# Experts' third token round: two experts of each four, over 64 tokens, on all four column strips

## What is computed

```python
logits = jnp.einsum('btd,de->bte', h, P['moe_router'][i])
probs = jax.nn.softmax(logits, axis=-1)
top_p, top_i = lax.top_k(probs, TOP_K)                      # TOP_K = 2
top_p = top_p / jnp.sum(top_p, axis=-1, keepdims=True)
gate = jnp.sum(jax.nn.one_hot(top_i, N_EXPERTS) * top_p[..., None], axis=-2)
hg = jnp.einsum('btd,edf->btef', h, P['moe_w_gate'][i])     # 8 x 1024 x 1792
hu = jnp.einsum('btd,edf->btef', h, P['moe_w_up'][i])       # 8 x 1024 x 1792
a = jax.nn.silu(hg) * hu * gate[..., None]
return jnp.einsum('btef,efd->btd', a, P['moe_w_down'][i])   # 8 x 1792 x 1024
```

## Time and profile before

| | |
|---|---|
| median of 3 runs | 1883.8 us (1882.7 to 1884.61) |
| profiled execution: its time, its span | 1880.36 us, 1878.4 us |
| TensorE busy | 1821.2 us, 97% of the span |
| VectorE, ScalarE, GpSimd busy | 34%, 19%, 8% |
| TensorE's granted clock, mean | 0.99 of full speed |
| DMA moved | 563.94 MB, 300 GB/s over the span |
| gather(0) to scatter(1) on TensorE | 1355.3 to 1870.6 us |

### The profile page before, as it was taken

How to read it: one execution, slowest core, us unless ns; L and a number is a source line. 1 busy time by engine, 2 the same in 40 slices (tenths; PEclk the granted TensorE clock), 3 DMA queues, 4 the chain that set the end, 5 groups by cost and what they waited for, 6 DMA issues and landing times.

```text
span 1878.4 us, 30169 instructions
## 1 busy us (share of the span) xinstructions
PE 1821.2 (97%) x12741; PEld 1295.9 (69%) x12741; DVE 644.2 (34%) x1394; ACT 366.0 (19%) x754; POOL 154.2 (8%) x259
## 2 busy tenths in 40 slices
PE   8999999999999999999999989999799999999998
PEld 5889888786688999888888878777433343433434
DVE  3444441527337665353544233452400000000000
ACT  2141333332000000015124332310110000100001
POOL 3000000404100110000000020320000000000000
PEclk9999999999999999999999999999799999999999
DMA  9933599989999998897349998997649999599992
GB/s 273 284 116 112 198 312 330 356 316 382 374 347 386 347 325 284 306 377 255 120 150 313 312 362 297 354 384 276 240 156 370 362 391 403 200 360 385 374 408 110
DMA packets 263162, 563.94 MB, mean 300 GB/s; under 512 B 11965, under 2 KB 160673, under 8 KB 262752
## 3 DMA queue, kind: packets, MB, share of 16 engines
q1 hardware_dynamic: 243696, 500.14, 74.1%
q0 software_dynamic: 18544, 58.58, 9.1%
q10 hardware_dynamic: 784, 3.25, 0.5%
HBM read 547.74 MB, written 196.63 MB: 396 GB/s over the span
## 4 chain that ended last, share of the span: by engine, by line
PE 93%; DMA 3%; DVE 2%; issue 1%; ACT 1%; POOL 0%; ACTq 0%; DVEq 0%; POOLq 0%
PE PS L902 33%; PE PS L1538 16%; PE PS L1564 8%; PE PS L1334 7%; PE PS L1310 4%; PE PS L1342 4%; PE PS L822 3%; PE PS L946 3%; PE PS L1324 2%; PE PS L1500 2%; PE PS L939 2%; PE PS L1586 1%; PE PS L1246 1%; PE PS L1220 1%; PE PS L837 1%
## 5 line engine op out<-in xcount | busy, mean ns | idle before, releaser
L902 PE MATMUL PS<-h,ring 128*128 128x264 f32 x2816 | 654.2, 389 | 0.0
L902 PEld LDWEIGHTS PS<-h,ring 128*128 128x128 f32 x2816 | 527.8, 191 | 106.8 <-issue 21.5
L1703 ACT COPY z<-PS 128x264 f32<-128x264 f32 (+3 forms) x307 | 130.6, 444 | 854.2 <-PE PS L902 527.8
L1538 PE MATMUL PS<-ring,z 128*32 128x512 f32 (+1 forms) x1440 | 212.2, 527 | 1.2 <-ACT z L1703 1.2
L1538 PE MATMUL PS<-arena,z 128*32 128x512 f32 (+1 forms) x1056 | 190.1, 535 | 0.0
L1538 PEld LDWEIGHTS PS<-ring,z 128*32 128x32 f32 x1440 | 68.5, 111 | 126.9 <-issue 111.4
L1564 PE MATMUL PS<-arena,z 128*32 128x512 f32 x432 | 104.0, 592 | 0.0
L1538 PEld LDWEIGHTS PS<-arena,z 128*32 128x32 f32 x1056 | 55.0, 110 | 53.5 <-issue 53.4
L1310 PE MATMUL PS<-z,ring 128*128 128x264 f32 x384 | 87.3, 388 | 0.0
L1538 PE MATMUL PS<-z 128*32 128x512 f32 x576 | 84.7, 593 | 0.0
L1564 PE MATMUL PS<-ring,z 128*32 128x512 f32 x480 | 83.5, 592 | 0.0
(11 more groups left out here) (357 smaller groups left out, 2192.4 us busy)
## 6 DMA issues: line engine op xcount, KB each, us to landing
out_win_s<-in_cache_win_kv SPq DMA_DIRECT2D x128, 1023.5 KB, 12.0
ring<-in_w_in SPq DMA_DIRECT2D x88, 1024.0 KB, 7.5
out_win_s<-in_cache_win_kv SPq DMA_DIRECT2D x32, 1022.0 KB, 12.4
ring<-in_moe_w_gate SPq DMA_DIRECT2D x28, 1024.0 KB, 9.6
arena<-in_moe_w_up SPq DMA_DIRECT2D x22, 1024.0 KB, 11.6
ring<-in_moe_w_up SPq DMA_DIRECT2D x22, 1024.0 KB, 8.8
ring<-in_moe_w_down SPq DMA_DIRECT2D x20, 1024.0 KB, 11.1
arena<-in_moe_w_down SPq DMA_DIRECT2D x18, 1024.0 KB, 10.4
```

The source lines that it names most:

```text
L902: last = mm(bank(l, "p", j)[:, 0:T], w[:, k, P * (j % 2):P * (j % 2) + P], h[:, k, :], start=(k == 0), stop=(k == KT - 1))
L1538: last = mm(m_bank("c", "gu", g, b, w, r)[BLK * j:BLK * j + BLK, 0:n], hs[:, k, P * r + BLK * j:P * r + BLK * j + BLK], v3(slot_ap(set_slo ...
L1703: return nc.scalar.copy(out, in_)
```

## The change

The first two rounds stay as they are (FULL = 64 tokens of each expert). The third serves only PAIR = 2 experts of the four, those with more than 64 tokens. Each of them gets two strips, one for the left and one for the right half of the weight columns, so that a third-round matmul has 256 columns (128 in the block of 256) in place of 512. In the down part its two output halves lie on two strips, in one PSUM bank (five `dn` banks in place of six). A group has SLOTS = 320 slots in place of 384.

Which two experts these are is known only at run time. VectorE reads their numbers into registers (`which`) and copies their part of each set, in two pieces of 1024 columns for each of the two, from the set's place to two fixed tiles `over[0]` and `over[1]` (`bring`); TensorE reads them there (`over_piece`). The semaphores `over_in` and `over_used` pass the tiles to and fro, one piece at a time. So that a register can address the chunk, the four chunks of a set now lie next to each other: ring and arena are one tile `mem`, and the third set place is in the tail of `z` (`set_slots`). The third round's turn-overs are two in place of four, ScalarE copies them in one or two parts (`turned`), and two ST tiles more are turned back, eight in all. In `route` VectorE also finds which experts are over 64 and whether more than two of a four are (then `crowded` is set too); `find_slots` and `weigh_slots` build G and `gw` with wide instructions.

Not shown below: new places of some tiles in memory, one semaphore in place of two for `relb_in` and for `r_gate`, the list of PSUM banks, and the order of ScalarE's `slots_back`.

```diff
+FULL = (ROUNDS - 1) * BLK
+PAIR = 2
+SLOTS = QUAD * FULL + PAIR * BLK
...
+        def unended(n):
+
+            ended = [t for t in range(SET_EG) if GU_SETS[t][2] != 0] + [SETS - 1]
+            return n - sum(1 for g in range(2) for t in ended if 2 * (SETS * g + t) + 1 < n)
...
+        ztail = z.rearrange("p a b -> p (a b)")[:, Z_N * T - QUAD * CW:Z_N * T]
...
+        def set_slots(t):
+
+            if t % 3 < 2:
+                return v3(mem[:, QUAD * (t % 3) * CW:QUAD * (t % 3 + 1) * CW], QUAD)
+            return v3(ztail, QUAD)
...
+        over = [small[:, 0:D], cm.take(D)]
...
-                            last = mm(m_bank("c", "gh", g, d + w)[:, 0:QUAD * CAP], htok[i][0:nt, P * (d + w):P * (d + w) + P],
-                                      G[0:nt, i, g].rearrange("p r j s -> p (r j s)"), start=(i == 0), stop=(i == 2))
+                            last = mm(m_bank("c", "gh", g, d + w)[:, 0:SLOTS], htok[i][0:nt, P * (d + w):P * (d + w) + P],
+                                      G[0:nt, i, g, :], start=(i == 0), stop=(i == 2))
...
-                for i in range(BLOCKS[b][1] // P):
+                for i in range(BLOCKS[b][1] // P // (1 if u % ROUNDS < 2 else PAIR)):
...
+            def over_piece(g, t, p, out, tokens, ks, kt):
+
+                n = 2 * (SETS * g + t) + p
+                pe.wait_ge(over_in, n + 1)
+                wide = out.shape[1]
+                for k in ks:
+                    for s_ in range(QUAD):
+                        a_, half = s_ // 2, s_ % 2
+                        last = mm(out[BLK * s_:BLK * s_ + BLK, :], tokens[:, k, QUAD * FULL + BLK * a_:QUAD * FULL + BLK * a_ + BLK],
+                                  v3(over[a_], len(ks))[:, k - ks[0], wide * half:wide * half + wide],
+                                  start=(k == 0), stop=(k == kt - 1))
+                        if k == ks[-1] and s_ == QUAD - 2 and t >= SET_EG and p == 1 and t < SETS - 1:
+                            last.then_inc(sets_used, 1)
+                return last
 
             def hidden_chosen(g):
...
-                    for r in range(ROUNDS):
+                    for r in range(2):
...
-                        if part == 0:
-                            continue
-                        last.then_inc(m_done("c", "gu", g, b, w, r), 1)
-                        if w and b + r:
-                            turn_hidden(g, ROUNDS * b + r - 1)
-                    if g == 0 and 2 <= t < 8:
+                        if part != 0:
+                            last.then_inc(m_done("c", "gu", g, b, w, r), 1)
+                            if w and b + r:
+                                turn_hidden(g, ROUNDS * b + r - 1)
+                        if not part and r == 0:
+                            m_open(pe, "c", "gu", g, b, w, 2)
+                        half = ks[r * len(ks) // 2:(r + 1) * len(ks) // 2]
+                        last = over_piece(g, t, r, m_bank("c", "gu", g, b, w, 2)[:, 0:n // 2], hs, half, KT)
+                        if part != 0 and r == 1:
+                            last.then_inc(m_done("c", "gu", g, b, w, 2), 1)
+                        else:
+                            last.then_inc(over_used, 1)
+                    if w and part != 0:
+                        turn_hidden(g, ROUNDS * b + 1)
+                    if g == 0 and 2 <= t < 10:
...
-                        for n in range(2 * ROUNDS):
+                        for n in range(4):
...
-                    if q < SET_ED - 1:
-                        last.then_inc(sets_used, 1)
+                        if k == 0:
+                            m_open(pe, "c", "dn", g, 4)
+                        last = over_piece(g, SET_EG + q, w, m_bank("c", "dn", g, 4), fc, range(k, k + 1), FE // P)
...
-                    for r in range(ROUNDS):
-                        last = mm(m_bank("c", "fd", g, d)[:, 0:T], ys[:, r, P * d:P * d + P], ST[:, ROUNDS * g + r, :],
-                                  start=(r == 0), stop=(r == ROUNDS - 1))
+                    out = m_bank("c", "fd", g, d)[:, 0:T]
+                    for r in range(2):
+                        mm(out, ys[:, r, P * d:P * d + P], ST[:, QUAD * g + r, :], start=(r == 0), stop=False)
+                    last = mm(out, ys_over[:, P * (d % 4):P * (d % 4) + P], ST[:, QUAD * g + 2 + d // 4, :],
+                              start=False, stop=True)
                     last.then_inc(m_done("c", "fd", g, d), 1)
...
+                if r == 2:
+                    n = n // P // PAIR
+                    for i in range(n):
+                        last = copy(fc[:, c0 // P + i:c0 // P + i + n + 1:n, QUAD * FULL:SLOTS].rearrange("p f (a s) -> p a f s", a=PAIR),
+                                    m_bank("c", "tf", g, u)[:, P * i:P * i + P].rearrange("p (a f s) -> p a f s", a=PAIR, f=2))
+                    last.then_inc(m_read("c", "tf", g, u), 1)
+                    return
...
+                counts = bank(1, "rc", 0)[:, 0:NE]
+                ts(rover, counts, float(FULL) + 0.5, None, ALU.is_gt)
+                link(nc.vector.tensor_reduce(rmost[:, 0:1], counts, AX.X, MAX))
+                dve.drain().then_inc(free(1, "rc", 0), 1)
+                ts(rmost[:, 1:2], rmost[:, 0:1], float(CAP) + 0.5, None, ALU.is_gt)
+                for g in range(2):
+                    last = nc.vector.tensor_tensor_scan(rorder[:, QUAD * g:QUAD * g + QUAD], ones[:, 0:QUAD],
+                                                        rover[:, QUAD * g:QUAD * g + QUAD], 0.0, MUL, ADD)
+                link(last)
+                link(nc.vector.tensor_reduce(rmost[:, 2:3], rorder, AX.X, MAX))
+                link(stt(rmost[:, 0:1], rmost[:, 2:3], float(PAIR) + 0.5, rmost[:, 1:2], ALU.is_gt, ADD))
+                ts(crowded[0:1, 0:1], rmost[0:1, 0:1], 0.5, None, ALU.is_gt).then_inc(r_flag, 1)
+                for a_ in range(PAIR):
+                    last = stt(rsel[:, a_].rearrange("p g j -> p (g j)"), rorder, float(a_ + 1), rover, ALU.is_equal, MUL)
...
+            def find_slots(g):
+
+                for r in range(2):
+                    tt(G[:, :, g, P * r:P * r + P].rearrange("p i (j s) -> p i j s", j=QUAD),
+                       ranks(1 + BLK * r).to_broadcast([P, 3, QUAD, BLK]),
+                       bc(rpos[:, :, QUAD * g:QUAD * g + QUAD], 3, [P, 3, QUAD, BLK]), ALU.is_equal)
+                over_rows(g, rpos)
+                tt(third(G[:, :, g, 2 * P:SLOTS]), ranks(1 + FULL).to_broadcast([P, 3, PAIR, BLK]),
+                   bc(rab, 3, [P, 3, PAIR, BLK]), ALU.is_equal)
+                dve.drain().then_inc(r_slots, 1)
+
+            def weigh_slots(g):
...
+            def weigh_slots(g):
+
+                link(nc.vector.memset(gw[:, :, g, 2 * P:4 * P], 0.0))
+                over_rows(g, rg)
+                for r in range(2):
+                    tt(gw[:, :, g, P * r:P * r + P].rearrange("p i (j s) -> p i j s", j=QUAD),
+                       G[:, :, g, P * r:P * r + P].rearrange("p i (j s) -> p i j s", j=QUAD),
+                       bc(rg[:, :, QUAD * g:QUAD * g + QUAD], 3, [P, 3, QUAD, BLK]), MUL)
+                for half in range(2):
+                    at = 2 * P + P * half
+                    tt(gw[:, :, g, at:at + P].rearrange("p i (a f s) -> p i a f s", a=PAIR, f=2)[:, :, :, half, :],
+                       third(G[:, :, g, 2 * P:SLOTS]), bc(rab, 3, [P, 3, PAIR, BLK]), MUL)
+                dve.drain().then_inc(r_back, 1)
 
...
+                which = [[dve.value_load(crowded[0:1, 1 + 2 * a_ + g:2 + 2 * a_ + g], min_val=0, max_val=QUAD - 1)
+                          for a_ in range(PAIR)] for g in range(2)]
+
+                def bring(g, t, p):
+
+                    n = 2 * (SETS * g + t) + p
+                    if p == 0:
+                        for j in range(QUAD):
+                            s_ = set_slot(t, j)
+                            dve.wait_ge(landed[s_], 16 * (loads[s_] + (SETS * g + t) // 3 + 1))
+                    before = n - 1
+                    if before >= 0:
+                        g_, t_, p_ = before // (2 * SETS), before // 2 % SETS, before % 2
+                        if p_ and t_ == SETS - 1:
+                            m_wait_full(dve, "c", "dn", g_, 4)
+                        elif p_ and t_ < SET_EG and GU_SETS[t_][2] != 0:
+                            m_wait_full(dve, "c", "gu", g_, *GU_SETS[t_][0:2], 2)
+                        else:
+                            dve.wait_ge(over_used, unended(n))
+                    for a_ in range(PAIR):
+                        last = cp(over[a_], set_slots(t)[:, bass.DynSlice(which[g][a_], 1), D * p:D * p + D].rearrange(
+                            "p a b -> p (a b)"))
+                    last.then_inc(over_in, 1)
+
+                def gate_up(g, u):
+
...
+                    w = BLOCKS[b][1] // (1 if r < 2 else PAIR)
...
+                bring(0, 0, 0)
                 for g in range(2):
-                    for u in range(ROUNDS * len(BLOCKS)):
```

(42 more changed lines are left out.)

105 lines of the change are left out of this document (60 added, 45 removed).

## The result

The changed kernel takes 1848.76 us in the median of four runs (1848.23 to 1849.26). The kernel before, run beside it on the same chip, takes 1883.25 us, and the ratio is 0.9827, with a 95% interval of 0.9815 to 0.9839. The profiled execution took 1848.23 us around a span of 1846.1 us. The forecast was 1855 us with 1847 to 1868 as its range, by transfers that become the limit.

The account below looks back on a forecast made before the run. TensorE was taken to set the pace, with DMA transfers within half a microsecond a set. Savings of 9.8 + 14.2 + 6.2 - 1.7 = 28.5 us gave 1851.9, plus 3.4 for the median 1855 us, range 1847 to 1868.

Parts of the forecast that it names:

- What bounds the kernel: Expert part: TensorE sets the pace, but transfers have no room either; the two limits stand within half a microsecond a set.
- The transfers' chain: Hidden and down parts: group time built from first issue, transfers and last set; saves 14.2 us in group 0, 9.8 in group 1.
- TensorE's 73 us: All 42 sets: the gain at 1.74 us a set were TensorE alone the limit; with gathers 1804 us, a rival given 2%.
- The lighter set: Each weight set: half-width third-round matmuls cut TensorE's time by 1.74 us to 8.72 us.
- Gather: Both gathers: 320 columns in place of 384, at 290 ns an instruction, save 6.2 us (5.6 to 6.6).
- VectorE: Four new copies per set: a pair fits under TensorE's main round of 3.49 us, so they cost 0.
- the upper row: VectorE's copies: upper bound of 1.15 us a copy, read from a TENSOR_TENSOR operation at 1.08 ns an element.
- the lower row: VectorE's copies: lower bound of some 0.8 us a copy, read from a TENSOR_SCALAR of 128x528 taking 436 ns.
- C: TensorE in the sets: half clock does not end; 1910 us at 12.2 us a set; 4%, 6% more for a part.
- D: Staging tiles: a copy pair over 4.5 us stalls TensorE; gain gone at 4.9, 1929 us at sets of 12.7; 4%.
- The clock: TensorE after waits in each set: half clock shows only in a group's last set, 1.7 us; half of two, +1.7 us.
- The signs named ahead: Profile after: DMA waits of 1 to 2.5 us in most sets, about 25 a group; DMA idle between groups about 12.

Follow-up runs that it names:

- e1: Changed kernel with only the first half of each expert weight chunk transferred, all computation kept: 1798.57 us, ratio 0.9581.
- e2: Kernel before the change with only the first half of each expert weight chunk transferred: 1877.57 us, ratio 0.9985.
- e5: Changed kernel with each pair of VectorE copies made three times in a row: 1859.91 us, ratio 0.9894.
- e3: Changed kernel without VectorE's copies, TensorE reading the two experts' chunks in place at addresses written into the program: 1847.25 us, ratio 0.9822.
- e6: Changed kernel with each pair of VectorE copies made four times in a row: 1975.32 us, ratio 1.0521.
- e11: The changed kernel itself, measured again for comparison on one chip: 1846.87 us, ratio 0.9825.
- e7: Changed kernel with the scatter of group 0 spread, one tile behind each of sets 1 to 8 of group 1: 1837.01 us, ratio 0.9778.
- e10: The same kernel as e7, measured again beside the changed kernel on the same chip: 1839.12 us, ratio 0.9782.
- e8: Changed kernel with each gather cut in two, half before the group's first set and half behind it: 1844.12 us, ratio 0.9803.
- e9: Changed kernel with both the spread scatter of group 0 and the two gathers cut in two: 1839.60 us, ratio 0.9791.
- e4: Changed kernel without VectorE's copies and with only half of each expert weight chunk transferred: 1799.75 us, ratio 0.957.

## Why the prediction was right, point by point

*What bounds the kernel.* Shown: by e1 against e2 the change is worth 79 us without the transfers' limit and 35 with it, and while a group loads the DMA share stays at 1.04.

*The transfers' chain.* Forecast for group 1: 9.6 + 1.6 + 194.7 + 8.9 = 214.8 us. Measured: the first issue at 1622.68, which is 9.6 after 1613.08; bytes from 1624.3, 1.6 later; 192.9; then 9.03, in sum 213.15. Group 0 has 11.3 + 1.6 + 193.1 + 9.0 = 215.0 where 216.5 was forecast. What was off is the rate, above all that of the gate and up sets, 392 in place of 384 GB/s, and that is 3.1 us in both groups together. Why it rose is open. It is not that TensorE now waits: e5, where a set takes 10.5 us and TensorE waits for no DMA, has 391. Nor is it the copies, since e3 has 393 without them. The chunks also lie at new places in memory, and that was not tried alone. That the sum came out of the DMA's own chain, and not out of TensorE's 73 us, made the forecast.

*The lighter set.* 8.72 us was forecast, 8.58 measured. In the 256-column block the pieces of 128 columns cost less again (32 in 1.01 us), which I had left open; as said, nothing hangs on it.

*Gather.* 290 ns an instruction were read off the line between 264 and 384 columns; 14.48/48 = 302 ns were measured in gather(1), above the proportional 296 too. Gather(0) saved 1.9 us, as it again ran at half clock at first. Both gave 4.4 of the 6.2 us, below the 5.6 to 6.6 of the forecast.

*VectorE.* Cost zero, as forecast. I took the upper row, 1.15 us; a copy is 0.69, below even the 0.8 of the lower row. The Trainium skill says that an operation with one source in SBUF uses both read ports and goes twice as fast even in fp32, which one with two tensors can't ("VectorE: DVE Perf Modes", Mode 2×_2P); the trace agrees in kind, with 0.67 ns an element here against 1.08 in the earlier trace rows, 1.6 times as fast and not twice. The page would have named the lower row as the near one. It decides nothing at one pair, but by the upper row the three pairs of e5 would have taken 6.9 us, more than the 5.3 of e6's four.

*The prices of C and D.* They are some 25 us too low. By their figures, 1910 for sets of 12.2 us and 1929 for 12.7, both take 1855 us for a set of 10.9 and add from there. But the kernel before has sets of 10.84 us on average (455.3/42), so at 10.9 only the gathers' gain is left. Summed as for e5, sets of 12.7 give 42 x 12.7 = 533 us, 78 more than 455.3, less 6.2 for the gathers: 1956. D would have begun to lose near 11.0 us a set, a pair of 4.6 us and not 4.9, and part of the gain goes well before, as e5 shows at 4.0. The forecast doesn't use these prices, and it stands.

*The clock.* +1.7 us was forecast, none came. Windows of the kernel after, behind three of the waits for DMAs and, in the last row, at the begin of hidden(0), behind 1.2 us for ScalarE:

```profile
1670.00:1673.00 3.00, 3.00 (x19) 0.90 (x15) 0.61 (x2) 0.00 (x0) 0.00 (x0) 0.51 1.05 385
1735.00:1738.00 3.00, 2.49 (x24) 1.35 (x28) 1.63 (x3) 0.00 (x0) 0.00 (x0) 0.50 1.09 346
1496.00:1499.00 3.00, 2.62 (x28) 1.44 (x32) 1.62 (x3) 0.00 (x0) 0.00 (x0) 0.50 1.10 348
1372.70:1376.00 3.30, 3.30 (x20) 1.24 (x24) 0.00 (x0) 0.53 (x1) 0.00 (x0) 0.56 0.03 5
```

Of the 25 waits for DMAs the granted clock fell to 0.50 behind three, which had left TensorE idle for 2.14, 3.15 and 2.59 us (in the order of the rows); none of them came before a group's last set. That was luck as far as the term goes, which gave it an even chance. The wait that the prediction read this term from, 1.2 us before hidden(0), was one for ScalarE's copies. The round at 1669.35 took 5.34 us in place of 3.57, and the transfers hid it, as the forecast said they would. The Trainium skill shows a long wait for a DMA ahead of each round's matmuls as what puts TensorE at half clock ("TensorE: Matmul & The Clock Gate", Loop structure matters more than you think). The trace shows it behind three of the 25 waits, the three longest. Length alone doesn't sort all cases, as the 1.2 us before hidden(0) were enough. Rival C did not come about.

*The sum.* For the profiled execution 28.5 us were forecast and 32.1 came: +3.1 from the transfers' rate, +1.7 from the clock, +0.7 from an earlier gather(0), -1.8 from gather. The rest of the 6.5 us between 1855.3 and 1848.8 is the offset of the median over the profiled run, taken as 3.4 and now 0.5. No step failed; the mis-sized terms are these, the transfers' rate and the offset above all. The gathers' error hid part of the rate's, which is luck, and the offset is one of medians and nothing of the kernel.

*The signs named ahead.* The waits are 0.7 to 3.1 us long, but 16.1 and 19.4 us a group where about 25 was forecast. The work between the sets fills the rest: without any wait for a DMA group 1 takes 187.9 us in e1, 7.7 more than 21 sets of 8.58, and the forecast of the waits had left that out. The DMA's idle stretch between the groups fell from some 26 to 15.8 us (1608.5 to 1624.3), not to 12. A rate other than 384, 351 and 404 GB/s was named as a sign of being wrong; 392, 357 and 404 came, a small departure to the good. The distrust that the rate might fall once VectorE reads the slots was answered by e3.

## What to carry to other kernels

Where two limits stand within a few per cent, price a relief of one by the chain of the other: when its first transfer starts, how long it runs saturated, and what follows its last byte. Halving the transferred bytes of both kernels tells in two runs how much of a relief the transfers swallow; read it stage by stage, since here 5 of the 79 us came from elsewhere. When you price a slower helper, count also the stretches that the main limit does not pace, the first and the last sets. The rest is won where the DMA is idle: work ahead of the first release of a buffer is worth moving if it can be spread so thin that every later release still comes before the queue runs dry; moved in one piece, it only moves the gap.

## What the runs showed of the hardware

*A stretch of TensorE work can stay at half clock from end to end.* gather(0), 48 instructions of 320 columns behind the idle time of the branch, takes 16.9 to 17.1 us in the profiles of after, e3, e6 and e11, where its clock rises after some 5 us. In those of e7 and e10 it does not rise at all, and in that of e5 it rises only at the end, 27.3 us in all; the chain of waits of e10:

```profile
1342.56 7.72 issue
1350.27 28.03 PE PS L1530 x48
```

and its windows:

```profile
1350.30:1355.30 5.00, 5.00 (x9) 2.96 (x10) 3.92 (x12) 0.00 (x0) 0.00 (x0) 0.50 0.35 129
...
1365.30:1370.30 5.00, 5.00 (x10) 2.79 (x9) 0.00 (x0) 0.04 (x1) 0.00 (x0) 0.50 0.00 0
1370.30:1378.30 8.00, 7.99 (x14) 3.75 (x13) 0.00 (x0) 1.24 (x3) 0.00 (x0) 0.50 0.00 0
```

TensorE is busy throughout, with no transfer under way after the first 5 us, and still at 0.50. In e8 the first half gather took 14.03 us at 0.50 and the main round behind it 6.04, in the fastest execution of e9 9.76 at a mean of 0.74 and 3.64. For the whole gather it costs 11 us, in full, since the first release waits for it. The spread scatter is not what makes it slow, as e5 and e8 have none; whether it makes the slow case more frequent is not shown. The table fits: within e7 and within e10 the executions are, nearly in order, the slower the lower their mean clock, from 1835.4 us at 0.988 to 1848.1 at 0.981. Five of the six of e9 lie at 0.983 to 0.986 and the one whose gather is seen to recover at 0.989, 6 to 10 us below them; that the five had a slow gather is inferred from the clock, not seen. What decides it stays open.

*Idle time at a branch depends on the DMA's load.* Ahead of gather(0) the chain has 7.7 to 7.8 us of issue in the profiles of the changed kernel and all its variants with whole transfers, and from 1340 to 1350 us the DMA share is 1.05 in the kernel after. With half the transfers the weights are in before the branch and the share is 0.10 in e1 and 0.05 in e4; the issue is 2.82 and 4.90 us. gather(0) begins at 1349.3 there, and at 1349.8 to 1354.6 in the others, where the routing ahead also ends at different times. The kernel before has 3.19 us of issue before its last slot building, and 0.54 in e2. The only packets in e1 from 1342 to 1350 us are those of two queues that the profile calls "instruction", six with 0.07 MB. In the kernel after, from 1347 to 1354.6, four such packets stand among 1519 of weights, on the same 16 engines. That the instructions behind the branch queue up behind the weights would explain the idle time; no run tried it.
